# Weight loads of a two-layer decoder kernel, issued as two transfers of 64 partitions each

## The reference

```python
# layer 0
h = rms(x, e_norm); proj = h @ e_w_in            # 2048 -> 6144
u, z_s5, q, k, v, z_da = split(proj)             # six parts of 1024
y_s5 = s5_mixer(u, ...) * silu(z_s5)             # diagonal state space scan, then a 1024x1024 GLU
y_da = diff_attention(q, k, v, ...) * silu(z_da) # 8 heads
x = x + concat(y_s5, y_da) @ e_w_out             # 2048 -> 2048
# layer 1
h = rms(x, o_norm); proj = h @ o_w_in            # 2048 -> 8208
q, k, v, z, f_logit = split(proj)
y = forgetting_attention(q, k, v, f_logit) * silu(z)   # 16 heads
x = x + y @ o_w_out
```

## Time and profile before

| | us |
|---|---|
| median of 3 runs | 1111.54 |
| the profiled execution's own time | 1110.78 |
| its span, first to last instruction | 1109.1 |
| TensorE busy | 1034.5 |
| VectorE busy | 712.4 |
| ScalarE busy | 575.2 |
| GpSimd busy | 313.8 |
| weight queue (q1), share of the 16 DMA engines | 46.7% |

### The profile page before, as it was taken

The page is one execution under the profiler, slowest core; times in us unless marked ns, Lnnn a source line. Parts: engine busy times, 40 slices in busy tenths (PEclk is TensorE's granted clock), DMA queues, the critical chain, the costliest instruction groups (busy, mean ns, idle before and its releaser), DMA issues.

```text
span 1109.1 us, 14954 instructions
## 1 busy us (share of the span) xinstructions
PE 1034.5 (93%) x4957; PEld 827.5 (75%) x4957; DVE 712.4 (64%) x1036; ACT 575.2 (52%) x971; POOL 313.8 (28%) x288
## 2 busy tenths in 40 slices
PE   7799998798988979888999999999999999999998
PEld 7789865565655646567888887888788778878886
DVE  5494788788888979956655465455545555645543
ACT  5434563665555565465544555544554554555331
POOL 1000387846955965730000021012002100300000
PEclk9899998889888979889999999999999999999999
DMA  7845533322322232243665765545466754544562
GB/s 268 174 146 179 157 115 95 114 77 92 98 95 92 86 106 76 97 169 114 189 188 182 177 165 153 167 157 200 138 169 162 175 169 155 194 153 157 195 210 93
DMA packets 112729, 163.49 MB, mean 147 GB/s; under 512 B 19125, under 2 KB 52010, under 8 KB 112426
## 3 DMA queue, kind: packets, MB, share of 16 engines
q1 hardware_dynamic: 98256, 159.41, 46.7%
q10 hardware_dynamic: 14426, 3.48, 1.7%
HBM read 160.76 MB, written 2.10 MB: 147 GB/s over the span
## 4 chain that ended last, share of the span: by engine, by line
PE 65%; POOL 16%; DVE 8%; issue 7%; ACT 1%; DMA 1%; ACTq 1%; DVEq 0%; POOLq 0%; SPq 0%
PE bank L419 16%; PE bank L420 16%; PE bank L421 16%; POOL scr L1844 3%; PE bank L440 3%; PE bank L442 3%; PE bank L441 3%; POOL scr L1836 3%; POOL scr L1843 3%; POOL scr L1837 2%; POOL scr L1845 2%; POOL scr L1846 2%; DVE wl L854 1%; PE bank L554 1%; POOL con L1853 1%
## 5 line engine op out<-in xcount | busy, mean ns | idle before, releaser
L854 DVE TENSOR_TENSOR wl<-raw,wh 128x1024 fp32r<-128x1024 f32 x296 | 366.3, 1240 | 278.6 <-ACT wh L846 277.7
L846 ACT ACTIVATE wh<-raw 128x1024 fp32r<-128x1024 f32 x296 | 310.9, 1055 | 183.0 <-PE bank L421 133.4
L419 PE MATMUL bank<-wh,xh 128*128 128x512 f32 x768 | 320.8, 418 | 0.0
L420 PE MATMUL bank<-wl,xh 128*128 128x512 f32 x768 | 307.0, 400 | 0.0
L421 PE MATMUL bank<-wh,xl 128*128 128x512 f32 x768 | 305.9, 398 | 0.0
L419 PEld LDWEIGHTS bank<-wh,xh 128*128 128x128 f32 x768 | 148.3, 193 | 54.5 <-issue 22.3
L421 PEld LDWEIGHTS bank<-wh,xl 128*128 128x128 f32 x768 | 148.2, 193 | 33.9
L420 PEld LDWEIGHTS bank<-wl,xh 128*128 128x128 f32 x768 | 148.7, 194 | 27.3
L1861 POOL TENSOR_TENSOR con<-con 128x4 f32<-128x4 f32 x16 | 22.0, 1375 | 313.0 <-DVE con L1614 312.5
L419 PE MATMUL bank<-wh,yh 128*128 128x512 f32 x256 | 101.6, 397 | 4.1 <-ACT scr L1218 3.6
L420 PE MATMUL bank<-wl,yh 128*128 128x512 f32 x256 | 100.4, 392 | 0.0
(11 more groups left out here) (289 smaller groups left out, 1408.7 us busy)
## 6 DMA issues: line engine op xcount, KB each, us to landing
raw<-in_o_w_in SPq DMA_DIRECT2D x128, 512.0 KB
raw<-in_e_w_in SPq DMA_DIRECT2D x128, 256.0 KB
raw<-in_e_w_in SPq DMA_DIRECT2D x32, 512.0 KB
raw<-in_e_w_out SPq DMA_DIRECT2D x32, 512.0 KB
raw<-in_o_w_out SPq DMA_DIRECT2D x32, 512.0 KB
raw<-in_s_w_glu SPq DMA_DIRECT2D x8, 512.0 KB
res<-in_x SPq DMA_DIRECT2D x4, 512.0 KB, 7.9
res<-in_x SPq DMA_DIRECT2D x1, 2048.0 KB, 8.5
```

What stands on the lines that cost most here:

```text
L419: nc.tensor.matmul(o, l_hi, w_hi, start=first, stop=False)
L420: nc.tensor.matmul(o, l_hi, w_lo, start=False, stop=False)
L846: nc.scalar.activation(wh[:, j % RING, :], raw[:, j % RING, :], ACT.Copy).then_inc(hi_done, 1)
L854: nc.vector.tensor_tensor(wl[:, j % RING, :], raw[:, j % RING, :], wh[:, j % RING, :].bitcast(F32), ALU.subtract).then_inc(lo_done, 1)
```

## The change

In the branch for three dimensions the single DMA becomes two, of partitions 0 to 63 and of 64 to 127, 256 KB each, one directly behind the other on the same queue. Each counts 16 on the semaphore that had 32 before, so the conversion's wait stays as it was. The branch for four dimensions is not touched.

```diff
                 dst = raw[:, j % RING, :]
                 if len(src.shape) == 3:
-                    sp.dma_start(dst.rearrange("p (k n) -> p k n", k=src.shape[1]), src).then_inc(raw_in[j % RING], 32)
+                    dst = dst.rearrange("p (k n) -> p k n", k=src.shape[1])
+                    for lo in (0, 64):
+                        sp.dma_start(dst[lo:lo + 64], src[lo:lo + 64]).then_inc(raw_in[j % RING], 16)
                 else:
```

## The result

The changed kernel takes 1116.65 us (median of 5 runs, 1115.68 to 1117.51) against 1111.6 us (5 runs) before: ratio 1.0047, 95% interval [1.0032, 1.0061]. It is 5.05 us slower. The forecast was 1112.4 with a range up to 1115.8.

What follows compares the result with a forecast made beforehand. Mean bandwidth was taken to bind nothing; only awaited landings matter. x1 +0.6 and unit 21 +0.3 gave +0.9 us on 1111.54, so 1112.4, range 1110.8 to 1115.8.

Steps and rivals of the forecast that it cites:

- the stall of ScalarE's queue: ScalarE's issue standing 5.30 us at 32.25 us while small transfers drain beside weight loads; the forecast's sum had no term.
- slower rival: First 18 us, ScalarE's queue near 32 us, unit 21: halves move at half rate, 1114.7, up to 1117; chance 0.30.
- 2 x 0.4 = 0.8: ScalarE's issue at 32.25 us waits 0.8 us longer if the two weight loads beside the small transfers take longer.
- The bound: Whole kernel: mean bandwidth binds nothing, FoX's DMA engines are at 0.55; what matters is where a landing is waited for.
- reckoned cover of 5.6 us: FoX's fullest stretch, unit 223: 5.6 us lie between a late load and TensorE, so cost 0.
- Issues: SP's queue, 464 issues for 232: 0.75 us a unit in place of 0.40, hidden by SP's waiting, cost 0.
- the pair of 128 partitions: Two 256 KB transfers issued at 144.78 us, landed in some 3.0 us; taken to show two issues cost no more than one.
- Quiet queue: A unit's landing with little else queued, priced at unit 21: +0.3 us, between -0.03 and +0.8.
- unit 21 is 0.03 us from being the last to arrive: At 75.7 us ScalarE's conversion ends 0.03 us before VectorE's L1404, so any further load delay reaches TensorE.
- Full queue: At the start, unit 0 ahead of x1 on the same queue: x1 lands 0.6 us later, between 0 and 1.05.
- the second rival: Where the skill's port rule was said to lead; by list order everything hidden, 1111.5, chance 0.18.
- Behind x1: Units 1 to 3 at the start: 1.7 us covered for unit 1, similar room for units 2 and 3, cost 0.

Runs made afterwards that it cites:

- the experiment on units 12 to 31: Units 12 to 31 loaded as two halves of 64 partitions, all others whole, against the kernel before: 1110.93 us against 1111.61, ratio 0.9998.

## Why the prediction was wrong

**The step that failed: the stall of ScalarE's queue.** The forecast looked only for engines that wait for the weight loads themselves, and put at nothing what slower loads do to the other queue on the same DMA engines. It gave no reason for that. The slower rival had the term, as "2 x 0.4 = 0.8". The stall grew by 4.65 us. The 0.4 per load was the surplus of a unit alone in the queue. But there the small transfers are 8192 pieces of 64 bytes on the same engines. Between 30 and 45 us of the changed kernel their queue takes 71.6% of the 16 engines' time and the weight queue 53.0%, more than a whole together. ScalarE's issues stand until the small pieces drain: the last of the 8192 starts at 37.4 us before and at 44.0 after, and the issue behind them ends at 37.55 and at 44.24. In the traces, with whole units two loads lie beside them (units 10 and 11; unit 9 has landed at 27.6, before b_re goes out at 27.94). With units 8 to 11 as halves unit 9 lands at 29.2, just after b_re at 28.6. With the start late as well (units 0 to 11 as halves), unit 9 (issued at 26.9, landed at 32.7), 10 and 11 are all in flight behind b_re at 30.0: three slow loads beside the small packets in place of two fast ones. This third load is argued, not shown, and it can account for the 0.7 us in the two issues at most; why the rest of the excess arises behind unit 8 stays open.

**The bound: right.** Bandwidth in the mean binds nothing, and the FoX stage hides a DMA share that is 0.1 higher. In the changed kernel a stretch there runs at 0.98 of the engines and TensorE stays busy. How much of the reckoned cover of 5.6 us was used, no run measures:

```profile
870.00:874.00 4.00, 4.00 (x19) 3.34 (x18) 3.40 (x5) 1.37 (x2) 1.99 (x2) 1.00 0.98 164
```

**Issues: hidden, but mis-sized.** 0.75 us a unit was taken from the pair of 128 partitions; it is 1.20. So x1 was issued at 2.72 us, not at 2.2. The even and odd halves, with the same issues, cost nothing in the median, so the cover held at the real size too.

**Quiet queue: over the upper end, and priced by a misread row.** Unit 20 of the changed kernel is issued at 70.98 and its data end in the window 74.40 to 74.90:

```profile
70.98 1.25 SPq L342 DMA_DIRECT2D raw<-in_e_w_in  x2
```

```profile
74.40:74.90 0.50, 0.50 (x7) 0.50 (x6) 0.02 (x1) 0.00 (x0) 0.00 (x0) 1.00 0.51 107
```

That is some 3.8 us where the single transfer of unit 21 took 3.2: +0.6, taken as +0.3. Unit 21 itself did worse. ScalarE's wait for it, which the prediction named as a sign (2.03 plus 0.8 at most), grew to 3.97, by 1.94 us; with one transfer for each row tile it was 2.70, so the pair isn't free there either. But the price was zero, because the step "unit 21 is 0.03 us from being the last to arrive" misread a row. The tile view of raw in the kernel before, up to 75.9 us, counts the conversions:

```profile
L846 ACT ACTIVATE wh<-raw x22: 1040/1060/1062, 7.3 to 74.7; 128x1024 fp32r<-128x1024 f32 x22
L854 DVE TENSOR_TENSOR wl<-raw,wh x19: 1162/1225/1226, 8.3 to 75.8; 128x1024 fp32r<-128x1024 f32 x19
```

VectorE's L854 behind L1404 was its nineteenth conversion, unit 18's, which ScalarE had finished at 66.86; unit 21's own started at 82.72, three conversions later. The changed kernel and the experiment on units 12 to 31 show that the delay reaches nobody. Where one line serves all units, count which one a row is before pairing it with another engine's.

**Full queue: mis-sized.** I took 0.6 for x1, "the middle, since nothing in this trace says which end is nearer". In the profiled execution it was 1.23, a little beyond the upper end of 1.05. One execution does not fix it: in the five experiments that load units 0 to 3 in the same way, TensorE's wait for x1 ends at 9.32 to 10.71 us, 0.3 to 1.7 us later than before, against 8.99 to 9.18 in the five with whole loads there. The rule that the Trainium skill states on this (SBUF — State Buffer, "Door 1: The DMA port swizzle") points to the upper end (the prediction gives its time to "the second rival" and means the slower one, the first of its list): 196 GB/s for partitions 0 to 63 against 328 for all, both at 1 MiB, is a ratio of 0.60. Here 255 against 383 GB/s is 0.67, in a window that also holds x's whole transfers, and the even and odd halves, which by the page's mapping reach all ports, have 365. That ports are the cause is the page's account. What the runs show is that the choice of partitions (with the rows of the matrix that go with them) decides the rate, and not the number of transfers, their width or their bytes. For x1 alone the longer issues may have a part, since the even and odd halves too end TensorE's wait 0.4 us later, in one trace.

**Behind x1: the spare was too small.** The forecast had 1.7 us of room for unit 1 and "similar room" for units 2 and 3, and put them at zero. Their low conversions are 2.0, 3.4 and 4.8 us late, and b_re goes out 2.04 us late, 0.8 more than x1's 1.23.

The sum as measured: x1 1.23 for the 0.6 of the forecast, the units behind it 0.8 for 0, the stall 4.65 for 0, unit 21 0 for 0.3: 6.7 us between the traces, 5.05 between the medians. The slower rival named the place and the stall, and its total (1114.7, up to 1117) was nearer. That is luck in part: its "up to 1117" rested on FoX, which cost nothing, and of its own terms unit 21 was 0.8 for 0 and the stall 0.8 for 4.65.

## What to carry to other kernels

Cut a load into its row tiles, not into partitions 0 to 63 and 64 to 127: two transfers over all partitions, or of even and odd ones, cost nothing here; the two blocks cost a third of the full-queue rate. A slower load costs only where a landing is waited for, and the place to look is not only who waits for the loads themselves but which other queue's issues stand behind the same DMA engines. A queue that stands for microseconds at an issue (5.30 us at one instruction here) is worth more than the transfers around it: moving two transfers of 64-byte pieces apart gained 6.4 us.

## What was not expected of the hardware

An issue of 64 partitions took longer than one of 128 with the same bytes and pieces: 599 ns (0 to 63) and 605 ns (even ones) against 333 ns for one row tile over 128 partitions, all 128 pieces of 2 KB (medians). For the GLU's loads the shortest was 465 ns for 64 pieces of 4 KB, against 352 ns for the whole unit of 128 such pieces. Why is open.

An issue can stand for microseconds behind earlier transfers of its own queue. Behind 4096 pieces of 64 bytes (s5_b_re) the equal s5_b_im stood 3.86 us in the kernel before; the small da_lambda_q, put in its place, stood 1.31 us with whole loads on the other queue and 5.80 us with halves (it came 2.5 and 1.35 us behind s5_b_re, where s5_b_im came 0.4 us behind it).
